# The roots of the norms from block two's output projection to the MLP, moved from ScalarE and VectorE to GpSimd

## The reference, cut to what matters

```
def layer_norm_2(x, g, b):                    # end of block two
    mu  = mean(x); var = mean(square(x - mu))
    return (x - mu) * rsqrt(var + 1e-5) * g + b

def rms_norm_3(x, g):                         # block three
    return x * rsqrt(mean(x * x) + 1e-6) * g

# block two, end:      x = layer_norm_2(ALPHA * x + (mixed @ w_out + b_out), ln_g, ln_b)
# block three:
h = rms_norm_3(x, norm_mix_g)
q, k, v, u, gate = split(h @ w_in)
q = rms_norm_3(q by head, q_norm_g);  k = rms_norm_3(k by head, k_norm_g)
a = sliding_window_gqa(q, k, v, sinks, rel_bias)          # window 128, 8 heads of 64
c = silu(layer_norm_3(causal_conv31(u * sigmoid(gate)), conv_ln_g, conv_ln_b))
mix = concatenate([rms_norm_3(a, attn_out_g), rms_norm_3(c, conv_out_g)])
x = x + mix @ w_out
h = rms_norm_3(x, norm_mlp_g)
x = x + square(relu(h @ w_mlp_up)) @ w_mlp_down
```

## Time and profile before

| what | us |
|---|---|
| median of 3 runs (lowest, highest) | 3580.22 (3579.59, 3581.22) |
| the profiled execution, its own time | 3576.74 |
| its span, first to last instruction | 3574.9 |
| busy: PE / DVE / ACT / POOL | 3162.6 / 2058.0 / 1199.2 / 435.5 |
| output projection of block two, 2206 to 2364: PE busy of 158 | 127.43 |
| gate, 2364 to 2495: PE busy of 131 | 124.02 |
| query, key and value, 2495 to 2585: PE busy of 90 / DVE busy | 83.48 / 74.04 |
| window attention, 2585 to 2708: PE busy of 123 | 92.50 |
| convolution norm, 2708 to 2742: PE busy of 34 | 10.52 |
| output projection of block three, 2742 to 2872: PE busy of 130 | 118.15 |

### The profile page before, as it was taken

One profiled execution on the slowest core, in us unless ns is written; L12 is line 12 of the kernel. 1 busy time (PEld: TensorE's weight loads), 2 busy tenths in 40 slices (PEclk: granted clock), 3 DMA queues, 4 the chain that ended last, 5 costly groups with the idle time before them and its releaser, 6 DMA issues. The chain is left out here.

```text
span 3574.9 us, 37584 instructions
## 1 busy us (share of the span) xinstructions
PE 3162.6 (88%) x14208; PEld 2408.6 (67%) x14208; DVE 2058.0 (58%) x3113; ACT 1199.2 (34%) x2280; POOL 435.5 (12%) x407
## 2 busy tenths in 40 slices
PE   6999889887688879989997886989876989999999
PEld 5787667665577768767885654444554478888887
DVE  5112544487588744839888984549854334444444
ACT  2211231587466642224124653000373011111111
POOL 2000002243011100221340022010000000000000
PEclk9999999997899999999998868999998999999999
DMA  6323126432733334341373412311101011111111
GB/s 218 135 72 101 44 75 200 142 118 80 189 90 95 95 120 155 118 108 30 112 215 115 121 68 88 118 58 57 47 1 62 0 47 48 47 48 48 54 52 59
DMA packets 189934, 326.63 MB, mean 91 GB/s; under 512 B 16242, under 2 KB 110610, under 8 KB 189754
## 3 DMA queue, kind: packets, MB, share of 16 engines
q1 hardware_dynamic: 168602, 250.29, 22.9%
q0 software_dynamic: 21152, 73.94, 5.8%
HBM read 233.71 MB, written 89.16 MB: 90 GB/s over the span
## 5 line engine op out<-in xcount | busy, mean ns | idle before, releaser
L215 PE MATMUL banks<-b3h4a_hi,b3mlpw_part 128*128 128x512 f32 x1024 | 318.8, 390 | 6.8 <-DVE b3mlpw_part L3280 6.8
L215 PE MATMUL banks<-b3mlpw_part,b3mlp_acthi 128*128 128x512 f32 x1024 | 315.2, 389 | 0.0
L215 PE MATMUL banks<-b1ln_w,b_hThi 128*128 128x512 f32 x768 | 238.4, 391 | 0.0
L215 PEld LDWEIGHTS banks<-b3h4a_hi,b3mlpw_part 128*128 128x128 f32 x1024 | 192.9, 188 | 47.2 <-issue 7.1
L215 PEld LDWEIGHTS banks<-b3mlpw_part,b3mlp_acthi 128*128 128x128 f32 x1024 | 192.2, 188 | 39.9
L3327 DVE TENSOR_TENSOR b3out_x<-b3out_x,banks 128x1024 f32<-128x1024 f32 x128 | 154.7, 1218 | 111.6 <-PE banks L215 111.6
L3297 ACT ACTIVATE b3mlp_relu<-banks 128x1024 f32<-128x1024 f32 x32 | 32.9, 1029 | 498.0 <-PE banks L215 498.0
L215 PE MATMUL banks<-b3out_lo,b3mlpw_part 128*128 128x512 f32 x512 | 199.7, 390 | 0.0
L215 PE MATMUL banks<-b3mlpw_part,b3mlp_actlo 128*128 128x512 f32 x512 | 199.2, 389 | 0.0
L508 PE MATMUL banks<-b_hThi,b1item_hi 128*128 128x512 f32 x464 | 195.9, 422 | 3.4 <-DVE b1item_lo L497 3.1
L508 PE MATMUL banks<-b_hThi,b1item_lo 128*128 128x512 f32 x464 | 183.7, 396 | 0.0
(11 more groups left out here) (417 smaller groups left out, 6754.5 us busy)
## 6 DMA issues: line engine op xcount, KB each, us to landing
qk_spill<-b1scan_qk SPq DMA_DIRECT2D x64, 256.0 KB, 2.8
b1att_k<-qk_spill SPq DMA_DIRECT2D x64, 256.0 KB, 8.0
b1out_ws<-in_w_out SPq DMA_DIRECT2D x16, 1024.0 KB, 5.0
b3mlpw_stage<-in_w_mlp_up SPq DMA_DIRECT2D x16, 1024.0 KB, 5.3
b3mlpw_stage<-in_w_mlp_down SPq DMA_DIRECT2D x16, 1024.0 KB, 4.8
b2h_stage<-in_w_in SPq DMA_DIRECT2D x30, 512.0 KB, 3.9
b1item_stage<-in_w_in SPq DMA_DIRECT2D x29, 512.0 KB, 4.8
b1ln_stage<-in_w_in SPq DMA_DIRECT2D x12, 1024.0 KB, 6.3
```

Of the source, the lines that this page charges most:

```text
L215: last = pe.matmul(out, x, y, start=i == 0, stop=i == n - 1)
```

## The change

All roots of these stages become one step on POOL, `tensor_tensor(x, x, half, pow)`, which gives x to the power -0.5. DVE's reciprocals behind them and ACT's square roots are gone, and with them the table loads that the square root had needed. In `pool_project` two powers stand ahead of each tile's store; the roots of block three stand in a new function, `pool_roots3`, between `pool_gate` and `pool_mlp`. The semaphores are the same ones; DVE waits at the same places, except that the wait of `norm_scale` and `square_scale` now ends directly in the scaling.

```
 def norm_scale(K, v, s, out, src, g, b):
-    K.vs.mark(v.reciprocal(s[:, 14:15], s[:, 14:15]))
     K.vs.mark(v.scalar_tensor_tensor(out, src, s[:, 12:13], g, ALU.subtract, ALU.mult))
...
 def square_scale(K, v, s, out, src, g):
-    K.vs.mark(v.reciprocal(s[:, 1:2], s[:, 1:2]))
-    v.wait_ge(K.vs.sem, K.vs.n)
     return v.scalar_tensor_tensor(out, src, s[:, 1:2], g, ALU.mult, ALU.mult)
...
-def root(a, x):
-    return a.activation(x, x, ACT.Sqrt)
...
 def act_project(K, p):
...
-        st = r - 1
-        if 0 <= st < ST:
-            a.wait_ge(S["pj_var"], o.n0 + st + 1)
-            root(a, K.stat[(2 * st) % 12][:, 14:15]).then_inc(S["pj_std"], 1)
-            a.wait_ge(S["pj_var2"], o.n0 + st + 1)
-            s = K.stat[(2 * st + 1) % 12]
-            root(a, s[:, 14:15] if o.b2 is not None else s[:, 1:2]).then_inc(S["pj_std2"], 1)
...
 def pool_project(K, p):
     g, S, o = K.g, K.S, K.project[p]
     for st in range(ST):
+        g.wait_ge(S["pj_var"], o.n0 + st + 1)
+        s = K.stat[(2 * st) % 12][:, 14:15]
+        g.tensor_tensor(s, s, K.half, ALU.pow).then_inc(S["pj_std"], 1)
+        g.wait_ge(S["pj_var2"], o.n0 + st + 1)
+        s = K.stat[(2 * st + 1) % 12]
+        s = s[:, 14:15] if o.b2 is not None else s[:, 1:2]
+        g.tensor_tensor(s, s, K.half, ALU.pow).then_inc(S["pj_std2"], 1)
         g.wait_ge(S["pj_h2"], o.n0 + st + 1)
...
+def pool_roots3(K):
+
+    g, S, m = K.g, K.S, K.m3n
+
+    def power(x):
+        return g.tensor_tensor(x, x, K.half.to_broadcast([P, x.shape[1]]), ALU.pow)
+
+    for st in range(ST):
+        g.wait_ge(S["q3_ms"], st + 1)
+        power(K.stat[st][:, 0:10]).then_inc(S["q3_root"], 1)
+    for st in range(ST):
+        g.wait_ge(*S.at("wn_ms", st + 1))
+        power(K.stat[(2 * st + 1) % 12][:, 1:2]).then_inc(S["wn_root"], 1)
+    for i in range(2):
+        g.wait_ge(*S.at("n3_ms", i + 1))
+        power(m.rs[:, i]).then_inc(S["n3_root"], 1)
+    for st in range(ST):
+        g.wait_ge(*S.at("o3_ms", st + 1))
+        power(K.stat[st][:, 1:2]).then_inc(S["o3_root"], 1)
...
 def act_qkv3(K):
...
-            a.wait_ge(S["q3_ms"], r + 1)
-            root(a, s[:, 0:10]).then_inc(S["q3_root"], 1)
...
 def dve_qkv3(K, taps):
...
         v.wait_ge(S["q3_root"], st + 1)
-        then(v.reciprocal(s[:, 0:10], s[:, 0:10]))
...
 def act_window(K):
...
-        u = r - 4
-        if 0 <= u < N and u % NH == NH - 1:
-            st = u // NH
-            a.wait_ge(*S.at("wn_ms", st + 1))
-            root(a, K.stat[(2 * st + 1) % 12][:, 1:2]).then_inc(S["wn_root"], 1)
...
 def act_norm3(K):
...
-        a.wait_ge(*S.at("n3_ms", i + 1))
-        root(a, m.rs[:, i]).then_inc(S["n3_root"], 1)
...
 def dve_norm3(K):
...
-    then(v.reciprocal(m.rs[:, 0], m.rs[:, 0]))
...
-    then(v.reciprocal(m.rs[:, 1], m.rs[:, 1]))
...
 def act_out3(K):
...
-            a.wait_ge(*S.at("o3_ms", st + 1))
-            root(a, K.stat[st][:, 1:2]).then_inc(S["o3_root"], 1)
...
 def gpsimd_program(K):
...
     pool_gate(K)
+    pool_roots3(K)
     pool_mlp(K)
```

More of the change, by code:

```diff
@@ L2886, in act_qkv3 @@
         if r < ST:
-            pair, s = K.pair[r % 2], K.stat[r]
+            pair = K.pair[r % 2]
             a.wait_ge(S["q3_mm"], r + 1)
```

## The result

The kernel after takes 3587.45 us (median of 22 runs, 3583.99 to 3593.17), the kernel before on the same chips 3582.4 (22 runs, 3578.11 to 3587.34). The ratio of the runs is 1.0016, with a 95% interval of 1.0010 to 1.0023: 5.7 us slower (3.6 to 8.2; the two medians alone differ by 5.1), where the prediction said 6.2. The slowdown is clear of noise, and less than the 0.2% that the prediction took for a measurable change.

What follows compares the result with a forecast made beforehand. PE, busy 88% of the span, was taken as the bound, so roots count only at certain places, mainly where PE waits. Terms 1.24 + 3.36 - 1.80 + 0.50 + 2.64 + 0.25 = +6.2 us gave 3586.4, range 3578.5 to 3590.5.

Steps and rivals of the forecast that it cites:

- Trips: From DVE's step before a root to the scaling behind it: 0.72 us for one column, 1.88 eight, 2.21 ten.
- Block two's projection, first and last tile: Two roots a tile, together 0.62 us longer, showing only at the first and last tile: +1.24 us.
- Query, key, value: Ten-column roots, trip 1.68 us longer a tile, showing at the first and last tile only: +3.36 us.
- The rival on TensorE's clock: Clock falls after PE's longer wait before the first query-key-value transposes: +7.9 us in all, 3588.1; chance 0.14.
- The middle tiles: Six query-key-value tiles between first and last: longer trip hidden behind PE, with 0.3 us to spare each.
- Window: Window attention: exponential 0.30 us earlier in tiles 1 to 6, -1.8; tiles 0 and 7 +0.5; together -1.3 us.
- Scores still 2.8 us apart: Sign in the profile after: PE's scores at a window norm keep their spacing of some 2.8 us.
- Convolution norm: Two eight-column roots, each standing alone, so the longer trips show whole, 1.27 and 1.37: +2.64 us.
- Block three's projection: Only the last tile's root shows, trip 0.72 in place of 0.47: +0.25 us.
- Contention: Rival: narrow powers on the path take 1.52 us, not 0.55, as beside DVE's scaling: +12.6, 3599.0; chance 0.06.
- Wide powers cheap: Rival: ten and eight columns cost what one does, 0.72 us: +0.9 in all, 3581.1; chance 0.11.

Runs made afterwards that it cites:

- contention experiment: Kernel after, with VectorE's first scaling step in block two's layer norm no longer waiting for the root, so the power runs beside it; 3585.2 us in one run.
- the two edited profiles: Kernel before with the next head's shift ahead of the scaling, 3582.22 us; kernel after with unread square roots bringing the window's table loads back, 3590.7 us.

## Why the prediction was right

- *Trips.* 0.66 to 0.69 us for one column, not 0.72; 2.06 for ten, not 2.21; 1.87 and 1.76 for eight, not 1.88. The line through two measured widths was 0.15 us too high at ten columns; that a power pays for its width is as predicted.
- *Block two's projection, first and last tile.* +1.24 predicted; by the trips (0.34 + 0.19 for a tile) it would be +1.1, the stages show +1.6. What is over goes with the clock behind the first wait, but the change isn't shown to be its cause: with roots the stage took 139.6 or 139.7 us in the five profiles with a clock of 0.84 or 0.85 there, and 140.4 and 140.3 in the two with 0.76; with powers 141.2 at 0.80 and 142.3 at 0.71. In the contention experiment, whose trips are 0.3 us shorter for each tile, it took 140.0 at 0.85: +0.4, where its trips give +0.5.
- *Query, key, value.* +3.36 predicted, +3.8 in the stages, of which the trips of the outer tiles give 3.1. The rival on TensorE's clock came true here in part: in four of the five profiles with powers the clock fell where it said, behind the first transposes, in none of seven with roots, and where one power stood there it cost 1.6 us (the rival had 1.7). The forecast left it out because 2.5 us is far less than 8.44; waits of 2.24 to 2.40 us were enough, and one of 3.09 went without. That the longer wait causes it is read from rows only, no run held the clock fixed. The middle tiles had 0.9 us to spare and not 0.3: I took DVE's free time as a mean over the stage, and it isn't even.
- *Window.* -1.3 predicted, -3.0 in the stages. The mechanism (the second load holds the exponential) was shown by the loads put back. The size was off in two ways: 0.36 for each tile and not 0.30, as the trip is 0.66; this makes -2.2 + 0.4 (tiles 0 and 7 pay 0.19 each and not 0.25). Of the rest, some 1.2 (0.7 without the two edited profiles), most is clock again: each of the four profiles with loads has one tile of 15.0 us among those of 14.07, with a clock of 0.89 over it, and the tiles of 13.71 have none such. Why it falls there isn't shown. "Scores still 2.8 us apart" was wrong: they come at 2643.62 and then at 2646.87, since PE's earlier scores run ahead and its transposes then wait for the scaled tile.
- *Convolution norm.* +2.64 predicted, trips +2.5, stages +3.0; the transposes of `b3norm_z` there take 364 to 383 ns in the mean in the five profiles with powers, and 337 to 358 in six with roots, 380 in the seventh. *Block three's projection:* +0.25 and +0.2.
- *Contention* stayed away because DVE waits for every power; the last experiment shows that its price is real where DVE doesn't wait. *Wide powers cheap* fell with the 1.96 and 1.65 us.

The mechanism held at every place, but that the sum of 6.2 came so near to 5.7 is in part luck: the terms that were too small (the window's gain, off by 1.2 to 1.7, and the clock's share in the other stages) have opposite signs.

## What to carry to other kernels

Price a moved scalar step by its trip (end of the step ahead to start of the step behind) and by its width, and count it only where the consumer already waits. Two table loads around a root cost what they push behind the next real dependence, 0.36 of 2.57 us here, and the larger gain of taking them away is the order that becomes possible: here, with the window's roots alone moved, 9.7 us for both, 4.3 for the powers alone and nothing for the order alone. On these numbers only narrow roots are worth sending to GpSimd, and only out of a stream that switches tables (one column 0.66 against 0.86 us where a load stood ahead of the root, 0.66 against 0.47 where none did; ten columns 2.06 against 0.53). When a consumer is moved, look at what an in-order TensorE has queued behind it.

## What the runs showed of the hardware

- GpSimd's power on 128 partitions: 0.55 us for one column, 1.65 for eight, 1.96 for ten; 1.53 for one column beside a DVE step with two SBUF inputs, 0.55 beside one that reads PSUM and SBUF.
- A trip from DVE to GpSimd and back is 0.1 to 0.2 us longer than its power.
- With a TensorE wait of some 2.2 us for the scaled tile in every window tile, the later part of the window had a clock of 0.66 to 0.98 in each stretch of 10 us; with waits of 0.72 us there it was 1.00. Behind a single wait of 2.24 to 2.40 us ahead of the query-key-value transposes it was 0.83 or 0.84 (three profiles), behind one of 3.09 it was 1.00 (one profile).
- Two table loads at a norm took 2.57 us of ScalarE's time and 0.36 us of the tile's.
